# Two attentions in one kernel: context tiles in one step, bands of 8 columns, outputs of two steps multiplied out together

## The reference, cut to what matters

```python
mask = (jnp.abs(qi[:, None] - kj[None, :]) <= A_WINDOW) & (kj >= 0)[None, :] & (kj < S)[None, :]
p = jax.nn.softmax(jnp.concatenate([s_lat, s_ctx, s_sink], axis=-1), axis=-1)
o = jnp.einsum('bkgqj,bjkd->bqkgd', p_lat, vb) + jnp.einsum('bkgqc,bckd->bqkgd', p_ctx, vc)
y = (o * jax.nn.silu(g)) @ w_out
oc = ctx_attention(qc.reshape(B, C, A_KV_HEADS, A_GROUPS, HEAD_DIM), kc, vc, sink_l)
```

```python
s = s + jnp.transpose(bias, (0, 2, 3, 1, 4))[None]
s = jnp.where(col_mask, s, NEG_INF_2).reshape(B, N_HEADS_2, n_cb, B_QW, kh * B_REG_W)
p = jax.nn.softmax(jnp.concatenate([s, s_ctx], axis=-1), axis=-1)
```

## Time and profile before

| | us |
|---|---|
| median of 3 runs | 2025.38 |
| lowest, highest | 2025.32, 2027.76 |
| the profiled execution | 2027.67 |
| its span, first to last instruction | 2025.8 |
| TensorE busy in it | 1973.2 |

### The profile page before, as it was taken

How to read it: one execution, slowest core, us unless ns; L and a number is a source line. 1 busy time by engine, 2 the same in 40 slices (tenths; PEclk the granted TensorE clock), 3 DMA queues, 4 the chain that set the end, 5 groups by cost and what they waited for, 6 DMA issues and landing times.

```text
span 2025.8 us, 36948 instructions
## 1 busy us (share of the span) xinstructions
PE 1973.2 (97%) x14892; PEld 1637.8 (81%) x14892; DVE 1074.9 (53%) x2229; ACT 825.6 (41%) x1639; POOL 829.3 (41%) x623
## 2 busy tenths in 40 slices
PE   7999999999999999999999999999999999999996
PEld 6888888888887888888888788778888888888785
DVE  5556556766855665556666733734334433434625
ACT  4110110110126566566677610745554555555601
POOL 3433333323345712222122625555445345344846
PEclk9999999999999999999999999999999999999998
DMA  4432322332221401110011423221111111111333
GB/s 160 135 99 85 107 95 83 107 102 84 94 93 65 157 12 45 35 35 22 25 35 36 135 91 115 76 90 53 43 53 53 42 53 53 43 52 53 110 120 135
DMA packets 51063, 156.02 MB, mean 77 GB/s; under 512 B 5584, under 2 KB 9296, under 8 KB 50768
## 3 DMA queue, kind: packets, MB, share of 16 engines
q1 hardware_dynamic: 49888, 152.40, 22.8%
q10 hardware_dynamic: 1008, 1.27, 0.2%
HBM read 132.94 MB, written 20.71 MB: 76 GB/s over the span
## 4 chain that ended last, share of the span: by engine, by line
PE 64%; DVE 4%; issue 2%; ACT 2%; POOL 1%; DMA 1%; DVEq 0%; SPq 0%; POOLq 0%; ACTq 0%
PE psum L924 16%; PE psum L926 14%; PE psum L925 14%; PE psum L1113 8%; PE psum L1060 6%; PE psum L1076 5%; PE psum L933 1%; POOL w_lo L738 1%; DVE prob_t L1838 1%; DMA w_raw<-weights_in 1%; ACT logits L1394 0%; DVE logits L1816 0%; PE psum L1087 0%; DVE u_lo L1693 0%; ACT u_tmp L1324 0%
## 5 line engine op out<-in xcount | busy, mean ns | idle before, releaser
L924 PE MATMUL psum<-u_hi,w_hi 128*128 128x512 f32 (+1 forms) x1440 | 544.8, 378 | 2.6 <-DVE u_lo L1693 2.6
L925 PE MATMUL psum<-u_lo,w_hi 128*128 128x512 f32 (+1 forms) x1440 | 525.4, 365 | 0.0
L926 PE MATMUL psum<-u_hi,w_lo 128*128 128x512 f32 (+1 forms) x1440 | 525.3, 365 | 0.0
L736 POOL CAST w_hi<-w_raw 128x1024 fp32r<-128x1024 f32 x140 | 157.4, 1124 | 818.8 <-DMA w_raw<-weights_in 818.8
L738 POOL TENSOR_TENSOR w_lo<-w_raw,w_hi 128x1024 fp32r<-128x1024 f32 x140 | 347.8, 2484 | 11.2
L924 PEld LDWEIGHTS psum<-u_hi,w_hi 128*128 128x128 f32 x1440 | 272.5, 189 | 54.9 <-DVE u_lo L1693 4.4
L926 PEld LDWEIGHTS psum<-u_hi,w_lo 128*128 128x128 f32 x1440 | 272.5, 189 | 44.9
L925 PEld LDWEIGHTS psum<-u_lo,w_hi 128*128 128x128 f32 x1440 | 273.1, 190 | 38.7
L1394 ACT ACTIVATE logits<-logits,neg_max 128x640 f32<-128x640 f32 (+2 forms) x288 | 226.0, 785 | 71.5 <-DVE neg_max L1816 70.0
L1403 ACT ACTIVATE logits<-logits,row_rec 128x640 f32<-128x640 f32 (+1 forms) x288 | 218.0, 770 | 0.0
L1417 ACT ACTIVATE prob_t<-psum 128x320 f32<-128x320 f32 (+1 forms) x288 | 118.7, 412 | 235.5 <-PE psum L1076 235.4
(11 more groups left out here) (164 smaller groups left out, 3037.3 us busy)
## 6 DMA issues: line engine op xcount, KB each, us to landing
w_raw<-weights_in SPq DMA_DIRECT2D x140, 512.0 KB, 3.5
w_ada<-w_ada_in SPq DMA_DIRECT2D x48, 512.0 KB, 3.5
residual<-act_buf SPq DMA_DIRECT2D x4, 2048.0 KB, 7.4
tab<-bias_tab_in SPq DMA_DIRECT2D x16, 496.5 KB
res<-residual SPq DMA_DIRECT2D x26, 256.0 KB, 3.4
y_all<-staged SPq DMA_DIRECT2D x24, 256.0 KB, 4.7
act_buf<-x_t_in SPq DMA_DIRECT2D x8, 512.0 KB, 13.3
staged<-a_y SPq DMA_DIRECT2D x6, 640.0 KB, 3.0
```

The source lines that it names most:

```text
L736: pool.tensor_copy(w_hi[:, slot, :], w_raw[:, slot, :]).then_inc(w_hi_done, 1)
L924: pe.matmul(out, wh, xh, start=first, stop=False)
L925: pe.matmul(out, wh, xl, start=False, stop=False)
L926: return pe.matmul(out, wl, xh, start=False, stop=last)
```

## The change

- First layer: the two context tiles are one step of four key tiles (twice the context keys, once for each half of the queries), so a pair has nine steps. ScalarE and VectorE treat the two halves with an instruction each.
- Second layer: a tile of queries is a band of 8 columns over all 16 rows. Queries, keys and values are kept band by band, so that the keys of a tile are two or three whole bands (the tiles at both edges have four key tiles, the others five), one contiguous range; 10 tiles of values are turned instead of 18, two at a time. The gate chunk is half the columns of every row, not half the rows.
- Bias: three kinds, each with its own place; the table is divided by the query scale once, one sum of table and mask for each band.
- Both: outputs of two steps are multiplied out in every second step, one behind the other in one bank (a context step alone), and gated together. The turned probabilities have a third slot.
- First layer: the first three steps of a pair get 1.22 shares of the projection, the others less; the last pair is cut for nine steps.
- SP: the table and mask of the second layer are loaded after the first attention's last gated output; y for the last pair of the second layer is loaded in threes behind the parts of the last gate chunk.

```diff
+PROB_SLOTS = 3
...
+BAND = P // ROWS
+LAT_KEYS = 3 * P
 KEYS = LAT_KEYS + C
 KEY_TILES = KEYS // P
-TAB_R, TAB_C = 23, 63
-TAB_RUN = TAB_R * TAB_C - (7 * TAB_C + 15)
-TAB_ROWS = 16
-B_BUILDS = 6
-
-LAST_BIAS_USE = ((1, 6), (1, 7), (0, 0), (0, 2), (0, 3), (0, 4))
-
-
-TILES = (S // P + C // P, S // P)
+TAB = 2 * ROWS - 1
+TAB_RUN = (ROWS - 1) * TAB + ROWS + BAND
+BIAS_FIRST = (0, -1, -1)
+MASK_AT = (0, 2 * P, 5 * P)
+B_BUILDS = 3
...
+V_TILE, V_TURNS, V_TILES = (0, 3), (2, 2), (S // P + C // P, S // P + C // P)
...
+EARLY_PARTS = 3
...
+        done = (past + t / 2) / total
+        part = cut[min(parts - 1, int(done / (1 + early) * parts) if done < (1 + early) * EARLY_PARTS / parts else
+                       int(EARLY_PARTS + (done - (1 + early) * EARLY_PARTS / parts) / (1 - (1 + early) * EARLY_PARTS / parts) * (parts - EARLY_PARTS)))]
...
+    return parts + ([[(b0, 0, 6)], [(b0, 6, 7), (b1, 0, 7), (third, 0, 2)], [(third, 2, 7)]],
...
+PARTS = tuple([in_parts(row, TILES[layer], (0.22, 0.0)[layer]) for row in STAGES[layer][1:-1] + [STAGES[layer][-1][:-1]]]
...
-                times[c.kind, c.pair] = tuple(min(n + d, last) for d in (1, 3, 4))
+                times[c.kind, c.pair] = tuple(min(n + d, TILES[0] - (2 if c.kind == "q" else 1)) for d in (1, 3, 4))
...
+        if t == CTX_TILE:
+            return P, [(P, S, C), ctx], [8, 9, 8, 9], 3 * P
...
+    def in_bands(rows, n):
+
+        return rows[:, 0:S].rearrange("p (b r c) -> p r b c", c=BAND, r=ROWS)[:, n * ROWS // 2:(n + 1) * ROWS // 2]
+
+    def by_rows(ap):
+        return ap.rearrange("p (r b c) -> p r b c", b=S // P, c=BAND)
+
+    def half_columns(rows, n):
+
+        return rows[:, 0:S].rearrange("p (r c) -> p r c", c=GRID)[:, :, n * GRID // 2:(n + 1) * GRID // 2]
...
+    def batch_of(layer, g):
+
+        first = g - (g - TILE0[layer]) % TILES[layer] % 2
+        t = (first - TILE0[layer]) % TILES[layer]
+        return [first] if t == CTX_TILE else [first, first + 1]
+
+    def batches_to(layer, g):
+
+        while g >= TILE0[layer] and g != batch_of(layer, g)[-1]:
+            g -= 1
+        return max(g + 1, TILE0[layer])
+
+    def prob_of(layer, g, h):
+
+        slot = g % PROB_SLOTS
+        return (a_third, b_third)[layer][h] if slot == PROB_SLOTS - 1 else prob_t[:, slot, h]
+
     def out_bank(layer, g):
 
-        aside = 0 <= g - (TILE0[layer] + (PAIRS - 1) * TILES[layer] - 1) < 3
-        return (pj[EARLY[layer][0].index % 2][:, 0:P], True) if aside else (ps_out, False)
+        aside = 0 <= batch_of(layer, g)[-1] - (TILE0[layer] + (PAIRS - 1) * TILES[layer] - 1) < 3
+        t = (g - TILE0[layer]) % TILES[layer]
+        lo, hi = (0, 2 * P) if t == CTX_TILE else (t % 2 * P, t % 2 * P + P)
+        return (pj[EARLY[layer][0].index % 2][:, lo:hi], True) if aside else (bank(3)[:, C + lo:C + hi], False)
...
+            return buf[:, t * P:(t + 1) * P] if t < CTX_TILE else buf[:, S:TC]
+        return buf[:, :].rearrange("p (r c) -> p r c", c=GRID)[:, :, t * BAND:(t + 1) * BAND]
...
         def load_y(layer, loaded, spans, chunks):
 
-            sp.wait_ge(pj_done, chunks)
             sp.wait_ge(y_stored, 16 * STAGED * (layer + 1))
+            if chunks is not None:
+                sp.wait_ge(pj_done, chunks)
             for k in range(STAGED):
+                if chunks is None and k % 3 == 0:
+                    sp.wait_ge(late_part, k // 3 + 1)
                 for t0, tn in spans:
                     sp.dma_start(y_all[:, k, t0:t0 + tn], staged[layer][k, :, t0:t0 + tn]).then_inc(loaded[k], 16)
...
+            if layer == 0:
+                sp.wait_ge(gated, TILE0[1])
+                for h in range(2):
+                    load_tab(sp, 0, h)
+                sp.dma_start(b_mask[:, :], a["b_mask"]).then_inc(mask_loaded, 16)
...
+            lo = 0 if b == 1 else P
...
+                for g in range((LAT_KEYS - lo) // P):
+                    at = (1 - BIAS_FIRST[b] - g) * BAND
+                    ins = pool.tensor_tensor(dst[:, g], tab[h][:, :, at:at + BAND][:, ::-1, ::-1], mask[:, g], ALU.add)
+                ins.then_inc(bias_ready, 1)
...
+            for i, (c, k0, n) in enumerate(key_span(t)[1]):
+                at, q0 = score_column(layer, t, c), (t + i if ctx_queries(layer, t) else t) * P
...
+        def outputs(layer, batch):
+
+            pair, t, s = steps_of(layer, batch[-1])
             pe.wait_ge(pt_act, s + 2)
             pe.wait_ge(pt_dve, s + 2)
-            if g:
-                pe.wait_ge(gated, g)
-            out, aside = out_bank(layer, g)
-            if not aside and (layer == 1 or (t + 2) % TILES[0] < S // P):
+            if batch[0]:
+                pe.wait_ge(gated, batch[0])
+            if not out_bank(layer, batch[0])[1] and (layer == 1 or (t + 2) % TILES[0] != CTX_TILE):
                 pe.wait_ge(logit_done, min(s + 6, STEP0[layer] + 2 * PAIRS * TILES[layer]))
             elif t == TILES[layer] - 1:
                 after(pe, pj_free[EARLY[layer][0].index % 2], EARLY[layer][0].index // 2)
-            if t == 0 and pair == 0:
+            if batch[0] == TILE0[layer]:
                 for c in CHUNKS[layer]["t", 0]:
                     consumed(pe, c)
-            if layer == 0:
-                v, tiles = av[pair // 4], a_tile(t)[2]
-            else:
-                v, tiles = bv[pair % 2], [t % 4 * 4 + t // 4 + n for n in range(3)] + [16, 17]
-            for c, tile in enumerate(tiles):
-                for h in range(2):
-                    r = slice(h * HD, (h + 1) * HD)
-                    mm = pe.matmul(out[r, :], v[:, tile, r], prob_t[:, g % 2, h, c, :], start=c == 0,
-                                   stop=c == len(tiles) - 1)
-            mm.then_inc(pv_done, 1)
+            for g in batch:
+                pair, t, _ = steps_of(layer, g)
+                v, tiles = (av[pair // 4], bv[pair % 2])[layer], key_span(t)[2]
+                out = out_bank(layer, g)[0]
+                for c, tile in enumerate(tiles):
+                    first, last, at = c == 0, c == len(tiles) - 1, 0
+                    if ctx_queries(layer, t):
+                        first, last, at = c % 2 == 0, c % 2 == 1, c // 2 * P
+                    for h in range(2):
+                        r = slice(h * HD, (h + 1) * HD)
+                        mm = pe.matmul(out[r, at:at + P], v[:, tile, r], prob_of(layer, g, h)[:, c, :], start=first, stop=last)
+                mm.then_inc(pv_done, 1)
...
+                            if layer == 1 and part[2] < KT:
+                                mm.then_inc(late_part, 1)
...
+                if g > first and g - 1 == batch_of(layer, g - 1)[-1]:
+                    outputs(layer, batch_of(layer, g - 1))
...
+            if ctx_queries(layer, t):
+                row = lg[:, c0 - 1:c0 + C]
+                act.activation(row, row, ACT.Exp, scale=-1.0, bias=neg_max[:, n, 1:2], accum_out=row_sum[:, n, 1:2])
+                c0 += C
...
+            if ctx_queries(layer, t):
+                pr = logits[n][:, c0 - 1:c0 + C - 1]
+                act.activation(pr, pr, ACT.Copy, scale=row_rec[:, n, 1:2])
+                c0 += C
...
+            if g >= PROB_SLOTS:
+                act.wait_ge(pv_done, g - PROB_SLOTS + 1)
...
+                if t == CTX_TILE:
+                    mid = c0 + C
+                    step(dve.tensor_copy(logits[n][:, mid - 1:mid], start))
+                    dve.wait_ge(score_done, s + 1)
+                    dve.tensor_tensor_reduce(logits[n][:, c0 - 1:mid - 1], ps_score[h][:, score_column(0, t, c0):score_column(0, t, mid)],
+                                             a_mask[:, m0:m0 + C], -1.0, start, ALU.add, ALU.min, neg_max[:, n, 1:2])
+                    c0 = mid
...
+            dve.wait_ge(pv_done, batch_of(layer, g)[-1] + 1)
...
+                if g > first and g - 1 == batch_of(layer, g - 1)[-1]:
+                    for done in batch_of(layer, g - 1):
+                        gate_output(layer, done)
```

More of the change, by code:

```diff
@@ L219, with in_parts @@
 UNIT_END = unit_ends()
-def in_parts(row, parts):
+EARLY_PARTS = 3
+def in_parts(row, parts, early=0.0):
     cost = [(c, k, c.tn * 0.00134 if c.kind != "t" else 0.11) for c in row for k in range(c.steps)]
@@ L259, in rope_times @@
 def rope_times(pair):
-    parts, last = PARTS[0][pair], TILES[0] - 1
+    parts = PARTS[0][pair]
     times = {}
@@ L1030, in work @@
                         w = slice(k * P, (k + 1) * P)
-                        mm = product(out[:, 0:c.tn], (w_hi[:, slot, w], w_lo[:, slot, w]),
-                                     (u_hi[:, k, c.t0:c.t0 + c.tn], u_lo[:, k, c.t0:c.t0 + c.tn]), n == 0, n == c.steps - 1)
+                        if layer == 1 and c.kind == "g":
+                            xs = half_columns(u_hi[:, k, :], c.n), half_columns(u_lo[:, k, :], c.n)
+                        else:
+                            xs = u_hi[:, k, c.t0:c.t0 + c.tn], u_lo[:, k, c.t0:c.t0 + c.tn]
```

(24 more changed lines are left out.)

252 lines of the change are left out of this document (108 added, 144 removed).

## The result

The changed kernel takes 2056.64 us (median of 4 runs, 2054.05 to 2058.14), the kernel before 2026.20 on the same chips: a ratio of 1.0148, interval 1.0130 to 1.0166. It is 30 us slower; 2019.2 was predicted, and 2035 was the upper end of the range.

The account below looks back on a forecast made before the run. TensorE was taken to bound the kernel (1973.2 of 2025.8 us busy). Work removed 34.6 us, less 25.6, 1 and 1.8 given back, left 6.2 us: 2019.2 us against the median of 2025.38, range 1999 to 2035.

Parts of the forecast that it names:

- context tiles: First attention, one step fewer in each of 8 pairs: 1.4 us a pair, 11.2 us saved.
- merges: Both attentions, two output groups put into one 64 times, each saving a 0.15 us group entry: 9.6 us saved.
- +1: First attention's last pair: savings ahead of TensorE's 2.05 us wait for y are waited out there, 1 us lost.
- what is late next: First attention: short steps without outputs wait for ScalarE or VectorE copies, 25.6 us given back, bounds 0 and 40.
- The gate's matmuls in runs of 32 columns: Second attention, 384 gate matmuls reading 32-column runs: no cost, bounds -1 and +2 us.
- Bands of 8 columns: Second attention: edge tiles save 6.9 us, less turning of values 5.6, fewer transposes at the layer's start 1.3.
- the first (short steps don't wait): Rival, first attention: ScalarE and VectorE have room, 25.6 falls to a third or less, 1993 to 2005 us; chance 0.20.
- The second: Rival: first-attention waits bring TensorE's clock down, up to 1.6 us each; ten give 2035 us, slower; chance 0.27.
- The late loads of the last pair: Rival, last pairs' loads: upper bounds taken together, 5 + 1.5 us, 2026 us; chance 0.08.
- the joining that does nothing: Rival: the double output group costs what it saves, for instance waiting for two gates; 9.6 less, 2029 us; chance 0.05.
- the signs of being right: Output groups 2.1 to 2.3 us; 1 to 2 us idle in first-attention steps; second-attention pairs 2.2 to 2.4 shorter; gate matmuls unchanged.
- the two named for being wrong: The first attention gets shorter, or the second is not 15 to 18 us shorter.

Follow-up runs that it names:

- p2: Changed kernel with 384 unused bytes per partition ahead of w_ada, so the moving operands lie 384 bytes past a multiple of 512, as before the change: 2032.23 us, ratio 1.0025.
- p3: Changed kernel with 128 unused bytes per partition ahead of w_ada, so the moving operands start 128 past a multiple of 512, like the weights: 2030.49 us.
- q2: p3 with the outputs of each first-attention step multiplied out by themselves again, the second attention still merged: 2019.29 us, ratio 0.9954.
- q3: p3 with the outputs of each second-attention step multiplied out by themselves, the first attention still merged: profiled span 2025.2 us.
- r1: Changed kernel with 128 unused bytes, single outputs in both attentions, and the gate from contiguous columns for pairs 0 to 6: 2008.97 us, ratio 0.9909.
- r2: r1 with the two removed small loads put back ahead of c_in's load, into unread buffers replacing the 128 unused bytes: 2005.86 us, ratio 0.9892.
- q1: p3 with the second attention's gate made from 512 contiguous columns instead of 16 runs of 32: 2029.76 us.

## Why the prediction was wrong

The step that failed first is in the sum: it has no term for where the buffers lie. The change takes the masks out and rounds to 128, and the part on the removed work looked at neither. The 384 bytes cost 24 to 26 us of the 37 missed, four times the gain forecast. The sign would have been wrong without them too: p2 is slower than the kernel before (1.0025, 1.0016 to 1.0034).

p3 is the change as it was meant: 2.9 us slower in span than the kernel before, where 6.2 faster was forecast. By the forecast's own terms:

- *First layer*: 0 forecast, 2.4 lost in p3; q2, q3 and r1 lie between 0.9 and 5.9. The clock goes with it: ahead of the first score it fell in no stretch in r1 (0.9), in one in p3 (2.4), in two in q3 (4.6), in three in q2 (5.9). The rest goes with the two small loads that no longer stand ahead of c_in's large one: in r1 the third part of x_lo is ready at 18.3 us, in r2, which has them back, at 15.5. That c_in then competes with x is the likely reason, not shown. The part on the change looked at no load of the start.
- *First attention*: the forecast is -11.2 (context tiles) -4.8 (merges) +25.6 +1 = 10.6 us longer; p3 is 7.7 longer. The mechanism and its place held: steps of 4.4 us, then an idle of 0.9, 1.3 and 1.5 us for a ScalarE or VectorE copy, where 1.15, 1.3 and 1.9 were forecast; the wait for the last pair's queries is 2.9, where 3.6 was. That the stage comes out so near is in part luck: the merges were to cost 21.8 net and cost 13.9 (q2 against p3), the context tiles were to save 11.2 and save 6.2. The pairs don't follow as well: pair 0 is 3.0 us shorter where it was to be longer, pair 6 is 4.3 longer and was to be 2.9.
- *Context tiles in one step*: q2 has them without the merges, and its first attention is 6.2 us shorter than before, against 11.2. Pair 4 is 0.77 shorter, not 1.4. Transposes, projection and outputs give 0.7, where 0.6 was forecast; the score groups give 0.1 (9.36 to 9.27), where 0.8 was. The forecast let a whole score group go, but its matmuls stay: the joined group takes 1.05 us, the two before it took 0.87 and 0.81. And two other groups of the pair grew, from 0.85 and 0.87 to 1.22 each; why is not shown.
- *The merges in the second attention*: 4.8 us saved by the forecast, 5.6 lost by q3, a miss of 10.4. The step that failed is "what is late next": I worked it out for the first attention only, and took the second as free of it because its projections are long. A step with 27 or 33 matmuls still lost its cover when the double group went, 0.5 to 0.6 us at a time, mostly to VectorE's copies. What stands ahead of those copies in VectorE's queue I did not take apart.
- *The gate's matmuls in runs of 32 columns*: taken at 0 with bounds -1 and +2, 4 us by q1. It was taken from scores of 384 columns, which took 0.34 us in runs and contiguous; for 512 columns against full weights the runs cost about 10 ns a matmul.
- *Bands of 8 columns*: -6.9 -5.6 -1.3 = -13.8 forecast, with 0 for the rest of the stage. r1, with neither merges nor runs in pairs 0 to 6, has a second attention 12.8 us shorter, and in it a fall of the clock in the last pair, at 1877, that the kernel before doesn't have. A pair went from 76.5 to 74.8, 1.7 for the 1.66 forecast (two edges of 0.43, and 0.8 of turning). This part was right.

Of the rivals, the first (short steps don't wait) is refuted by 23.0 us of waits. The second had the right side, by luck: the clock fell as rarely as before, in three stretches ahead of 1940 in either kernel. The late loads of the last pair did not show: from its first score to the end it is 154.7 us before and 153.5 in p3. Nor did the joining that does nothing: each double group saves its 0.14 us, and loses more through what it moves. Of the signs of being right, the output groups came out as said (2.12 and 2.34 us); the pairs of the second attention and the gate's matmuls did not. Of the two named for being wrong, the second came true, the second attention being 0.9 us shorter instead of 15 to 18.

## What to carry to other kernels

A change that adds or drops a small buffer moves every buffer behind it. Before judging anything else, compare the start-to-start time of the same matmul in a stage that the change doesn't touch; if it moved, pad until stationary and moving operand lie alike modulo 256, counting from the first address that the matmul reads, and measure the change from there. And before calling a microsecond or two a gain or a loss, count the falls of the clock in both traces. Two steps' work put together saves one entry on the engine that bounds, and takes from every second step the time in which the other engines caught up: look for that wait wherever a step is merged, long ones too. The version that results, r2, keeps the bands and the joined context tiles, drops the merges, and is 1.1% faster than the kernel before.

## What the runs showed of the hardware

The step of a 512-column fp32r matmul with new weights each time depends on where its two SBUF operands lie to each other: 226.7 ns alike modulo 256, 232 to 233 where they are 128 or 64 apart. Other distances were not tried. Groups of 20 matmuls of 128 columns take 1.24 us alike and 128 apart. The Trainium skill, SBUF — State Buffer, section "A bandwidth-pool intuition that's wrong", gives TensorE an independent read port for loading weights, beside the one for the moving operand. Taken to mean that the two reads never meet, it would leave no room for an effect of place; here there is one, of 6 ns in 227, and the measurement decides. Why it is so is not shown: no run separates a shared bank from another cause.

A moving operand of 16 runs of 32 columns costs 236.6 ns on average where its first address lies like the weights' modulo 256 and 239.8 where it lies 128 off (p3); the same matmuls with contiguous operands take 228.1 and 228.2 (q1). That scores of 384 columns cost the same either way does not carry over.

The stretch at half the clock (0.51 granted, 1.2 of 2.4 GHz) at 651.3 cost r2 about 1.5 us, within the 1.1 to 1.6 that the prediction read from the earlier trace rows.
